# Tiles for compression and modulation, squares added by GpSimd, and another order at the even layer's end

## The reference, cut to what matters

```python
def rms_norm(x, g):                      # norms 0..5, two for each layer
    return x * rsqrt(mean(x * x, -1) + EPS) * g

# layer 0 (even): h = norm 0;  x += concat(silu(layer_norm(conv(u))), gla(h)) @ ev_w_out
#                 h = norm 1;  x += peer_ffn(h)       (experts: gelu(h @ u.T) * gates @ v)
# layer 1 (odd):  h = norm 2;  x += fox_attention(h) @ od_w_out
#                 h = norm 3;  x += peer_ffn(h)
# last block:     mod = silu(c) @ ada_w + ada_b       # 1024 -> 6144, six vectors
#                 h = norm 4 * (1 + scale1) + shift1;  x += gate1 * (attentions(h) @ w_out)
#                 h = norm 5 * (1 + scale2) + shift2;  x += gate2 * (relu(h @ w1)**2 @ w2)

def compress_blocks(src, pos, w1, w2):   # for keys and for values, two heads of 64
    blk = src[:, idx] + pos              # 15 blocks of 32 positions
    return silu(blk.reshape(..., 32 * 64) @ w1) @ w2
```

## Time and profile before

| | us |
|---|---|
| median of 3 runs | 2398.96 (2397.2 to 2399.26) |
| the profiled execution, its own time | 2398.77 |
| its span, first to last instruction | 2396.9 |
| TensorE busy | 2367.5 (99%) |
| VectorE busy | 1711.6 (71%) |
| ScalarE busy | 1330.3 (56%) |
| GpSimd busy | 442.0 (18%) |

### The profile page before, as it was taken

One profiled execution on the slowest core, in us unless ns is written; L12 is line 12 of the kernel. 1 busy time (PEld: TensorE's weight loads), 2 busy tenths in 40 slices (PEclk: granted clock), 3 DMA queues, 4 the chain that ended last, 5 costly groups with the idle time before them and its releaser, 6 DMA issues.

```text
span 2396.9 us, 41643 instructions
## 1 busy us (share of the span) xinstructions
PE 2367.5 (99%) x16544; PEld 2189.4 (91%) x16544; DVE 1711.6 (71%) x3247; ACT 1330.3 (56%) x2520; POOL 442.0 (18%) x386
## 2 busy tenths in 40 slices
PE   8999999999999999999999999999999999999999
PEld 8899999999888888877999999998888878899999
DVE  7966999778777777666599977775555554747864
ACT  6665445766544444566544466665555554666643
POOL 4700000788200000010000038870000000001000
PEclk9999999999999999999999999999999999999999
DMA  7233555443577777732255554346555565234452
GB/s 282 80 135 114 184 185 178 149 132 126 193 264 265 259 255 264 273 141 97 98 187 184 184 168 132 127 130 210 193 193 193 193 218 219 111 114 168 176 192 72
DMA packets 93200, 421.82 MB, mean 176 GB/s; under 512 B 10296, under 2 KB 12880, under 8 KB 85072
## 3 DMA queue, kind: packets, MB, share of 16 engines
q1 hardware_dynamic: 92720, 418.82, 50.9%
q10 hardware_dynamic: 288, 0.34, 0.1%
HBM read 415.96 MB, written 3.16 MB: 175 GB/s over the span
## 4 chain that ended last, share of the span: by engine, by line
PE 93%; DVE 4%; ACT 2%; issue 1%; DMA 0%; ACTq 0%; DVEq 0%
PE PS L170 92%; ACT mem L181 1%; DVE mem L191 1%; DVE r_sl L191 1%; ACT r_sh L181 1%; PE PS L173 0%; DVE mem L199 0%; DVE mem L205 0%; ACT L188 0%; DMA mem<-in_v 0%; DMA cst<-in_cst 0%; DVE mem L211 0%; DVE mem L202 0%; ACT r_hhi L181 0%; DVE mem L195 0%
## 5 line engine op out<-in xcount | busy, mean ns | idle before, releaser
L191 DVE TENSOR_TENSOR r_sl<-mem,r_sh 128x1024 fp32r<-128x1024 f32 (+2 forms) x750 | 895.1, 1194 | 517.9 <-ACT r_sh L181 516.4
L181 ACT ACTIVATE r_sh<-mem 128x1024 fp32r<-128x1024 f32 (+2 forms) x750 | 768.7, 1025 | 521.6 <-PE PS L170 467.5
L170 PE MATMUL PS<-r_hhi,r_sh 128*128 128x256 f32 (+1 forms) x2832 | 718.9, 291 | 7.7 <-ACT r_sh L181 3.2
L170 PE MATMUL PS<-r_hlo,r_sh 128*128 128x256 f32 (+1 forms) x2704 | 668.1, 285 | 1.0 <-DVE r_hlo L199 0.9
L170 PEld LDWEIGHTS PS<-r_hhi,r_sh 128*128 128x128 f32 (+1 forms) x2832 | 542.9, 192 | 17.1 <-issue 9.6
L170 PEld LDWEIGHTS PS<-r_hlo,r_sh 128*128 128x128 f32 (+1 forms) x2704 | 518.6, 192 | 5.7 <-DVE r_hlo L199 3.1
L196 POOL TENSOR_SCALAR xT<-cst,mem 128x128 f32<-128x128 f32 x256 | 332.3, 1310 | 550.9 <-ACT mem L181 497.9
L170 PE MATMUL PS<-r_hhi,r_sl 128*128 128x256 f32 (+1 forms) x2832 | 401.2, 283 | 0.6 <-DVE r_sl L191 0.6
L181 ACT ACTIVATE mem<-PS 128x256 f32<-128x256 f32 (+26 forms) x558 | 185.1, 341 | 331.1 <-PE PS L170 330.7
L170 PEld LDWEIGHTS PS<-r_hhi,r_sl 128*128 128x128 f32 (+1 forms) x2832 | 366.6, 192 | 1.5 <-DVE r_sl L191 1.0
L170 PE MATMUL PS<-r_sh,r_ch 128*128 128x512 f32 x1024 | 276.5, 391 | 1.3 <-ACT r_sh L181 1.3
(11 more groups left out here) (169 smaller groups left out, 2616.1 us busy)
## 6 DMA issues: line engine op xcount, KB each, us to landing
mem<-in_u SPq DMA_DIRECT2D x256, 512.0 KB, 3.8
mem<-in_v SPq DMA_DIRECT2D x256, 512.0 KB, 4.4
mem<-in_w SPq DMA_DIRECT2D x16, 2048.0 KB, 7.9
mem<-in_ada SPq DMA_DIRECT2D x48, 512.0 KB, 4.2
mem<-in_in SPq DMA_DIRECT2D x9, 2048.0 KB, 7.9
mem<-in_wq SPq DMA_DIRECT2D x8, 2048.0 KB, 8.1
mem<-in_od_in SPq DMA_DIRECT2D x6, 2048.0 KB, 10.2
mem<-in_ev_in SPq DMA_DIRECT2D x5, 2048.0 KB, 13.6
```

The lines of the kernel that those rows point to most:

```text
L170: return self.did(self.e and self.e.matmul(out, lhsT, rhs, start=start, stop=stop, skip_group_check=skip))
L181: return self.did(self.e and self.e.activation(out, in_, func, **kw))
L191: return self.did(self.e and self.e.tensor_tensor(out, a, b, op))
```

## The change

1. *Norms 1, 3 and 5.* GpSimd adds the eight chunks of squares into chunk 0 (`squares_added`), and TensorE does one ones-matmul on the sum (`square_total`), called between the high and the low products of the second tile. `scale_ac` and what hangs on it move one tile later. For norm 1 GpSimd squares the odd chunks as well (in `even_po`).
2. *Even layer's end.* The mean stands behind n = 3 and the variance behind n = 5; three more taps ahead of a wait of VectorE; ScalarE's high parts of tiles 6 and 7 before the variance, low parts with them; the load of the Ln/Exp table goes from behind tile 8 to the end of the stage.
3. *Modulation.* `ada_sum` gets four buffers in `hT`. After each four pieces TensorE sums them: four matmuls with one column of ones as weights and 512 columns moving, output row 32m. ScalarE copies the four rows and writes them to DRAM with four DMAs; SyncE reads them back as [48 x 128] late in the odd layer, TensorE transposes them at the start of the last block, and one VectorE add gives `mod`.
4. *Compression.* Each of the 32 matmuls becomes two of 64 rows by 64 columns, one for each head, into two banks.

```diff
+    def squares_added(po, k, of):
+        for c in range(1, 8):
+            po.wait_ge("sq", k, c)
+            if c > 1:
+                po.wait_ge("sq_add", k, c - 1)
+            po.tensor_tensor(of[:, 0, :], of[:, 0, :], of[:, c, :], ADD).then_inc("sq_add", k, c)
+    def square_total(pe, k, of):
+        bank_wait(pe, 0)
+        pe.wait_ge("sq_add", k, 7)
+        pe.matmul(PS[:, 0, 0:256], ones, of[:, 0, :], True, True).then_inc("ss", k)
+        emptied[0] = ("ln", k)
@@ mm_T: between the high and the low products
+        if between:
+            between()
@@ even_po
+        for c in range(8):
+            if c % 2:
+                po.wait_ge(*x_ready(1, c))
+                po.wait_ge(*po.tensor_tensor(hT[:, c, :], xT[:, c, :], xT[:, c, :], MUL).then_inc("sqP", 1, c))
+            if c:
+                po.wait_ge("sq", 1, c - c % 2)
+                if c > 1:
+                    po.wait_ge("sq_add", 1, c - 1)
+                po.tensor_tensor(hT[:, 0, :], hT[:, 0, :], hT[:, c, :], ADD).then_inc("sq_add", 1, c)
@@ even_ac
-        hi(ac, EV_OUT[2])
-        hi(ac, EV_OUT[3])
-        hi(ac, EV_OUT[4])
+        for n in EV_OUT[2:6]:
+            hi(ac, n)
...
-        hi(ac, EV_OUT[5])
+        hi(ac, EV_OUT[6])
+        hi(ac, EV_OUT[7])
...
-        hi(ac, EV_OUT[8])
-        ac.ready(LNEXP)
         for n in EV_OUT[9:]:
             hi(ac, n)
             if n >= EV_OUT[10]:
-                square(ac, 1, n - EV_OUT[10])
+                if n % 2 == EV_OUT[10] % 2:
+                    square(ac, 1, n - EV_OUT[10])
                 gained_hi(ac, 1, n - EV_OUT[10], ghiv, lambda c: P("f0", c))
         hi(ac, EV_OUT[15] + 1)
         square(ac, 1, 6)
         gained_hi(ac, 1, 6, ghiv, lambda c: P("f0", c))
         gained_hi(ac, 1, 7, ghiv, lambda c: P("f0", c))
-        square(ac, 1, 7)
+        ac.ready(LNEXP)
@@ even_ve
-        some(8)
+        some(11)
         ve.wait_ge("orr", 0)
@@ peer_ac
+                if j:
+                    modulation_ac(ac, j - 1)
@@ modulation_pe, for every fourth piece
-                last = pe.matmul(PS[:, b, m:m + 1], ada_sum[:, 128 * m:128 * m + 128], ones[:, 0:1], True, True)
+                last = pe.matmul(PS[32 * m:32 * m + 1, g, :], ones[:, 0:1], ada_sum[m], True, True)
+        def modulation_ac(ac, j):
...
+            ac.wait_ge("ada_rows", g)
+            if g:
+                ac.wait_ge("ada_out", g - 1, 3)
+            for m in range(4):
+                d = ac.activation(ada_row[32 * m:32 * m + 1, :], PS[32 * m:32 * m + 1, g, :], COPY).then_inc("ada_row", g, m)
+            ac.wait_ge(*d)
+            for m in range(4):
+                at = 512 * (4 * g + m)
+                ac.dma_start(io["md"][at:at + 512].rearrange("(o n) -> o n", o=1), ada_row[32 * m:32 * m + 1, :]).then_inc("ada_out", g, m)
@@ peer_pe
-                    gained_block(pe, n, 1, (ghiv, glov), k, ("q", layer, 0, 0), (7,) if layer else (6, 7))
+                    gained_block(pe, n, 1, (ghiv, glov), k, ("q", layer, 0, 0), ())
...
-                    mm_T(pe, n, PS[:, (i + 1) % 4, 0:256], (ghiv, glov))
+                    mm_T(pe, n, PS[:, (i + 1) % 4, 0:256], (ghiv, glov), between=(lambda: square_total(pe, k, hT)) if i == 1 else None)
@@ last_ac
             hi(ac, W1[1])
+            hi(ac, W1[2])
             scale_ac(ac, 5)
             for i, n in enumerate(W1):
-                hi(ac, n + 2)
+                if i:
+                    hi(ac, n + 2)
@@ last_ve
-            ve.wait_ge("mod", 11)
+            ve.wait_ge("ada_turned", 0)
+            ve.wait_ge(*ve.tensor_tensor(mod, PS[:, 7, 0:48], P("adab"), ADD).then_inc("mod", 0))
@@ last_pe
+            pe.transpose(PS[:, 7, 0:48], ada_in, ident[0:48, 0:48]).then_inc("ada_turned", 0)
...
+                heads = ((slice(0, 64), 3 - a), (slice(64, 128), 6 + a))
                 for i in range(32):
-                    m = pe.matmul(PS[0:15, 3 - a, 0:128], blk[:, a, i, :], wi[:, i, :], i == 0, i == 31)
+                    for rows, b in heads:
+                        m = pe.matmul(PS[0:15, b, 0:64], blk[rows, a, i, :], wi[rows, i, rows], i == 0, i == 31)
```

More of the change, by code:

```diff
@@ L333, in build @@
     gw2, rr_ = small[0:16, 0:256], small[:, 256:512]
-    ada_sum = small[:, 0:512]
+    ada_sum = [hTf[:, 512 * i:512 * i + 512] for i in range(4)]
+    ada_row, ada_in = small[:, 0:512], small[0:48, 640:768]
     tbl, epst, onet = small[0:33, 512:520], small[:, 520:521], small[:, 521:522]
@@ L402, in build, with mm_T @@
     emptied = [None] * 8
-    def mm_T(pe, n, out, s, start=True, stop=True, after_norm=None, after=None, k0=0):
+    def mm_T(pe, n, out, s, start=True, stop=True, after_norm=None, after=None, k0=0, between=None):
         h, l = sh(n), sl(n)
@@ L548, in gained_block @@
         emptied[b] = evicted
-        square_sum(pe, k, sums[-1], squares)
+        if sums:
+            square_sum(pe, k, sums[-1], squares)
     def scale_ac(ac, k):
@@ L1037, in convolved_low @@
             ve.tensor_tensor(ylov[:, c, :], yT[:, c, :], hhiv[:, c, :].bitcast(F32), SUB).then_inc("ya_lo", c)
-        convolved_low(0)
-        lo(ve, EV_OUT[7])
-        for c in (1, 2, 3):
+        for c in range(4):
             convolved_low(c)
@@ L1319, in peer_ac @@
                 p, j = i // 4, i % 4
-                if i + 1 < len(qs):
+                if i + 1 < len(qs) and i != 1:
                     hi(ac, n + 1)
@@ L1599, in modulation_pe, with four_pieces @@
+        def four_pieces(j):
+            pc = (j - 4) // 10
+            if layer or j < 4 or pc >= 12 or pc % 4 != 3 or (j - 4) % 10 != 8:
+                return None
+            return pc // 4
         def modulation_pe(pe, j):
-            pc = (j - 4) // 10
-            if layer or j < 4 or pc >= 12 or (j - 4) % 10 != 8:
+            g = four_pieces(j)
+            if g is None:
                 return
-            b = pc % 4
-            bank_wait(pe, b)
-            pe.wait_ge("ada", pc, 3)
+            bank_wait(pe, g)
+            pe.wait_ge("ada", 4 * g + 3, 3)
@@ L2650, in compress @@
                 wi = wring[x.slot][:, 0:x.width].rearrange("p (i n) -> p i n", i=32)
-                bank_wait(pe, 3 - a)
+                heads = ((slice(0, 64), 3 - a), (slice(64, 128), 6 + a))
+                for _, b in heads:
+                    bank_wait(pe, b)
                 pe.wait_ge(f"w{x.slot}", x.g)
@@ L2847, in last_pe @@
                 emptied[c] = ("x", 4, c)
-                for x in range(2 if c == 2 else 1):
-                    square_sum(pe, 5, c - 2 + x + (c > 2), ma)
             pe.wait_ge("shift_cut", 0)
@@ L2853, in last_pe @@
                 if i == 0:
[L2854 removed]
+                    gained_block(pe, n, b, wide258, 5, ("scaled_w", 0), ())
                 else:
                     bank_wait(pe, b)
[L2857 removed]
+                    mm_T(pe, n, PS[:, b, 0:258], wide258, between=(lambda: square_total(pe, 5, ma)) if i == 1 else None)
                     emptied[b] = ("scaled_w", i)
```

74 lines of the change are left out of this document (41 added, 33 removed).

## The result

The changed kernel takes 2378.96 us (median of 4 runs, 2375.99 to 2380.68), the kernel before on the same chip 2398.08: ratio 0.992, 95% interval [0.9908, 0.9933], so 0.8% faster. The forecast was 2378, range 2371 to 2388. The profiled execution took 2375.99, 22.8 less than that of before.

The account below looks back on a forecast made before the run. TensorE, busy for 99% of the span, was taken as the bound. From 2398.77 us, -2.0 - 1.7 - 4.5 - 6.7 + 0.2 - 6.4 = -21.1 gave 2377.7, stated as 2378, range 2371 to 2388.

Parts of the forecast that it names:

- Compression and modulation: Compression calls 3.9 us each instead of 7.1, -6.4; modulation groups 1.1 each, -6.7 with ScalarE's lateness.
- ScalarE's copies: Modulation: four copies and four DMA issues per group make ScalarE some 0.3 late two tiles later; +0.9 for three groups.
- not side by side: Rival: strips and halves do not overlap; modulation +0.8, compression 0, the rest -8.0; 2391.6 us, chance 0.08.
- slower: Rival: compression records neither overlap nor shorten, +14.2, modulation in sequence too; sum +7.0, 2405.8 us, chance 0.04.
- Norm 3: Odd layer's end: six ones-matmuls fewer, -2.5, less 0.8 lost along the tiles to VectorE held by GpSimd; -1.7.
- Norm 5: Last layer: seven ones-matmuls fewer, -2.9, and a wait for VectorE in W1's third tile, +0.9; -2.0.
- The even end's front: Even layer's end, new order: mean starts 1.25 earlier, variance comes 2.9 earlier, TensorE 4.4 earlier by tile 11.
- I expect no fall of the clock after that: Even layer's end: with about 0.8 idle left before the mean, the mean takes 1.6 and not 2.3.
- Norm 1's tiles: Even layer's end: of 2.5 from six tiles' ones-matmuls, 1.2 kept beside GpSimd's one and a half operations per tile.
- Its tail: Norm 1 behind the last output tile: second WQ tile 0.7 later, one sum in it 0.4; +1.1.
- its high part ends about T+2.35: Norm 1's tail: chunk 7's high part ends 2.35 after the last output tile (T); second WQ tile starts T+4.65.
- first rival: VectorE, held by GpSimd, bounds the layers' ends: gives back 1.2 + 0.7, up to 1.4 at tails; 2381, chance 0.12.

Follow-up runs that it names:

- experiment 3: Changed kernel with the four one-row matmuls of each modulation group all in the first column strip, each into its own bank; 2385.84 us, ratio 0.9951.
- experiment 4: Changed kernel with modulation's one-row matmuls widened to 32 equal rows, then one copy and one DMA per group instead of four each; 2377.29 us, ratio 0.9912.
- experiment 5: Changed kernel with the low part of W1's third tile issued by VectorE ahead of its wait for the norm's root; 2378.86 us, ratio 0.992.
- experiment 1: Changed kernel with the compression's two heads one behind the other instead of in turns; 2386.82 us, ratio 0.9946.
- experiment 6: Changed kernel with ScalarE's table load moved from ahead of the second WQ tile's high part to just ahead of norm 1's root; 2376.94 us, ratio 0.9908.
- experiment 7: Changed kernel with all eight squares of norm 1 made by ScalarE, GpSimd only adding; 2377.65 us, ratio 0.9918.
- experiment 8: Changed kernel with norm 1's part undone: ScalarE squares all chunks, TensorE sums them by eight ones-matmuls; new order and load's place stay; 2377.51 us, ratio 0.991.
- experiment 9: Kernel before with only the even layer's end in the new order, table load between the high parts of tiles 10 and 11; 2395.32 us, ratio 0.9984.
- experiment 10: Changed kernel with the squares of norms 3 and 5 summed by TensorE again, norm 1 as changed; 2382.66 us, ratio 0.9933.
- experiment 11: Changed kernel with experiments 4, 5, 6 and 7 together, the eighth square behind the high part of WQ[1]; 2375.42 us, ratio 0.9898.
- experiment 12: Kernel of experiment 11 with unneeded matmuls filling TensorE's waits at the even layer's end; 2373.79 us, ratio 0.9904.

## Why the prediction was right, point by point

- **Compression and modulation** were priced from rows of other shapes and came within 0.2 us a call and 0.06 a group. The assumption that decided them, that halves and strips run side by side, was tested by taking the neighbourhood away: +6.7 and, in experiment 3's trace, +7.7. The "not side by side" and "slower" rivals are out.
- **ScalarE's copies** (+0.9): wrong in place. I had TensorE waiting two tiles later for ScalarE; it waited five tiles later, when ScalarE had itself waited for a weight piece. Beyond the groups (out: 12 x 0.95 with the slower start behind each; in: 3 x 1.19) the V phase lost 1.5 more to waits than before did, of which this wait and the slower start behind it are 0.85. Some of the others change place from execution to execution. Without the copies (experiment 4) this wait was gone and the phase was no shorter, so that the term was near in size is not shown to be more than luck.
- **Norm 3** (-1.7): -1.85, but not by the way forecast. The 0.8 that GpSimd was to cost along the tiles was not lost there: VectorE's subtractions took up to 0.62 for 0.48, and the tiles kept 1.44. What was lost came behind them, 0.5 of it in the wait for the high part of WQ[0]. The closeness of the number is in part luck. **Norm 5** (-2.0): -1.8, with the predicted wait of 0.9 at 0.86; experiment 5 showed its cause.
- **The even end's front** (-4.4): -4.1 in the profiled execution. The step "I expect no fall of the clock after that" failed. In 8 of the 12 profiled executions with the new order (the changed kernel's and experiments 1, 3 to 12) the clock was half for 3.4 us from about 131, behind the waits of 0.56, 0.54 and 0.29. From tile 9's start to tile 11's it is then 6.04 to 6.24 (experiments 6 to 9) and not 5.01: 1.0 to 1.2 lost, and 1.5 up to tile 12 in experiments 3 and 10 (7.94 and 7.95 for 6.45). The fall that stood at 119 is mostly moved, not removed. With it the change is worth -20.2 + 1.1 = -19.1, and the medians differ by 19.1; the profiled execution, the fastest of the changed kernel's four (2376.0, 2377.5, 2380.5, 2380.7), had neither this fall nor that near 2044.
- **Norm 1's tiles** (-1.2): -1.7. **Its tail** (+1.1): +2.2. The failed step is "its high part ends about T+2.35": it ended at T+3.1. I had left out that VectorE, which then has little slack per tile, arrives at T with a subtraction of the tile before still to do, and that GpSimd holds this one for 0.46. The other 0.3 is VectorE's own lateness. The Trainium skill (SBUF — State Buffer, "Who interferes with whom") says that such two exclude each other; 0.94 and 0.96 beside an addition, 0.48 without, agree. That is the first rival's mechanism, for 0.6 in the six tiles (9.26, and 8.64 without GpSimd's squares) and for 0.46 at the tail. The table load was a real cost there, as forecast, and free in two other places (experiments 6 and 9).
- The errors of the even end (+0.9), compression (-0.4), modulation (+0.4), norm 5 (+0.2) and norm 3 (-0.15) partly cancel: -21.1 against -20.2. That the median lies 1 us from the forecast is in part luck, since of the clock only the stretch at 119 was in the sum.

## What to carry to other kernels

Ask for each edit which engine stands right behind the bound one, and what it does at the tail of the stretch. Three edits of the same kind (sums taken from TensorE) gave 1.85, 1.8 and 0.2. Norm 3's output tiles are as short as norm 1's, 1.44, so the length of the tiles does not explain it; what norm 1 had besides was GpSimd's squares (0.55) and a table load on the chain of its tail (1.26), and without both, and with the last square moved, it gained 1.6. Price small matmuls by pairs that lie on different rows or strips, and issue them in turns; the same matmuls one head behind the other, or all in one strip, gain nothing (14.2 for 7.5; 3.60 for 1.04). Put a table load where its engine is ahead. Copying four one-row results by one instruction over all partitions took 0.60 of ScalarE's time and not 2.41, though the kernel's time does not show it.

## What the runs showed that I had not expected

- The granted clock differs between executions of the same program at the same waits. Behind identical waits (0.61, 0.56, 0.54 to 0.55, 0.29 to 0.30) near 117 to 129 it fell in experiment 5's execution and not in those of the changed kernel and of experiment 11. Stretches at 1.2 GHz were 3.4, 6.8 or 10.2 us long. 3.4 us of it cost 1.0 to 1.5 (1.1 near norm 4, 1.0 to 1.5 near 131, 1.5 near 2044), so effects of 1 us can't be read from medians of five.
- DMA issues by ScalarE differ widely: four of one row took 1.35 in all, one of four rows 1.06.
- Copying one partition of 512 columns took 0.60, as long as 128 partitions.
